# Moving squares, rows and factor sums from VectorE to GpSimd around the context part of a two-layer diffusion backbone

## What is computed

```
for layer in range(2):
    last = layer == 1
    sh1, sc1, g1, sh2, sc2, g2       = split(silu(c)     @ mod_w[layer] + mod_b[layer], 6)
    csh1, csc1, cg1, csh2, csc2, cg2 = split(silu(c_ctx) @ mod_w[layer] + mod_b[layer], 6)
    m_lat, m_ctx = mixer(...)                       # pooling + attention, then @ w_out
    h = h + g1 * m_lat
    f_lat = rmsnorm(h, norm_ffn_g) * (1 + sc2) + sh2
    h = h + g2 * ((silu(f_lat @ wg) * (f_lat @ wu)) @ wd)
    if not last:
        hc = hc + cg1 * m_ctx                       # the same for the context tokens
        ...
return h
```

## Time and profile before

| | |
|---|---|
| median of 3 runs | 3269.88 us (3264.45 to 3271.78) |
| the profiled execution's own time | 3270.94 us |
| its span, first to last instruction | 3268.8 us |
| PE busy | 3063.0 us, 94% of the span |
| POOL / DVE / ACT busy | 2193.1 / 1963.0 / 1089.5 us |
| mean granted TensorE clock | 0.968 of full speed |

### The profile page before, as it was taken

One profiled execution on the slowest core, in us unless ns is written; L12 is line 12 of the kernel. 1 busy time (PEld: TensorE's weight loads), 2 busy tenths in 40 slices (PEclk: granted clock), 3 DMA queues, 4 the chain that ended last, 5 costly groups with the idle time before them and its releaser, 6 DMA issues. The chain is left out here.

```text
span 3268.8 us, 44070 instructions
## 1 busy us (share of the span) xinstructions
PE 3063.0 (94%) x14302; PEld 2506.9 (77%) x14302; DVE 1963.0 (60%) x2625; ACT 1089.5 (33%) x1865; POOL 2193.1 (67%) x2250
## 2 busy tenths in 40 slices
PE   7998998989899999999798979999998999999999
PEld 6777876869777888888686757777776778888887
DVE  5585665787664454454435557777766765445454
ACT  4323675124530010110333446676772321010110
POOL 3584774520168888888633258888887688888884
PEclk9999998989899999999898979999998999999999
DMA  6367223458431111111212441111114211111112
GB/s 234 113 200 206 66 57 120 168 171 301 152 97 58 45 51 59 53 45 61 92 34 97 140 142 40 47 40 40 47 29 138 61 54 57 46 51 58 49 48 84
DMA packets 135064, 298.24 MB, mean 91 GB/s; under 512 B 36464, under 2 KB 69488, under 8 KB 134832
## 3 DMA queue, kind: packets, MB, share of 16 engines
q1 hardware_dynamic: 121776, 253.42, 24.7%
q10 hardware_dynamic: 13184, 43.52, 4.4%
HBM read 252.20 MB, written 44.63 MB: 91 GB/s over the span
## 5 line engine op out<-in xcount | busy, mean ns | idle before, releaser
L1546 POOL TENSOR_TENSOR a_pl<-a_p,a_ph 128x512 fp32r<-128x512 f32 x320 | 451.0, 1429 | 103.1 <-ACT a_p L1491 98.2
L164 PE MATMUL ps<-a_q,a_k 97*128 97x512 f32 x960 | 273.4, 398 | 1.2 <-POOL a_q L1565 1.2
L1490 ACT ACTIVATE a_ph<-ps 128x512 fp32r<-128x512 f32 x320 | 192.2, 601 | 178.8 <-PE ps L164 178.0
L1392 DVE TENSOR_REDUCE a_top<-ps 128x1 f32<-128x512 f32 x256 | 172.3, 687 | 95.3 <-PE ps L1316 95.3
L164 PE MATMUL ps<-hidden,whi 128*128 128x512 f32 x704 | 219.3, 393 | 5.0 <-issue 2.9
L164 PE MATMUL ps<-mixed_hi,l_whi 128*128 128x512 f32 (+1 forms) x544 | 208.9, 384 | 6.9 <-issue 2.9
L164 PEld LDWEIGHTS ps<-a_q,a_k 97*128 97x128 f32 x960 | 179.7, 191 | 38.2 <-issue 1.4
L2985 POOL TENSOR_TENSOR l_wlo<-l_raw,l_whi 128x512 fp32r<-128x512 f32 x154 | 199.4, 1295 | 12.8
L164 PE MATMUL ps<-mixed_lo,l_whi 128*128 128x512 f32 (+1 forms) x544 | 207.9, 382 | 0.0
L164 PE MATMUL ps<-mixed_hi,l_wlo 128*128 128x512 f32 (+1 forms) x544 | 207.8, 382 | 0.0
L3794 DVE SCALAR_TENSOR_TENSOR residual<-ps,mod,residual 128x512 f32<-128x512 f32 x176 | 132.0, 750 | 124.9 <-PE ps L164 124.9
(11 more groups left out here) (415 smaller groups left out, 8819.7 us busy)
## 6 DMA issues: line engine op xcount, KB each, us to landing
l_raw<-in_w_ffn SPq DMA_DIRECT2D x132, 512.0 KB, 3.7
raw<-in_w_ffn SPq DMA_DIRECT2D x66, 512.0 KB, 3.6
l_row<-in_mod_t ACTq DMA_DIRECT2D x48, 512.0 KB, 5.0
f_vraw<-in_mod_t ACTq DMA_DIRECT2D x24, 512.0 KB, 4.1
a_k<-scratch_k SPq DMA_DIRECT2D x32, 320.0 KB, 6.7
f_raw<-in_w_in SPq DMA_DIRECT2D x16, 512.0 KB, 5.4
l_raw<-in_w_out SPq DMA_DIRECT2D x16, 512.0 KB, 4.8
raw<-in_w_out SPq DMA_DIRECT2D x16, 512.0 KB, 4.5
```

Source lines behind the costliest of these rows:

```text
L164: last = nc.tensor.matmul(out, a, b, start=at == 0, stop=at == n - 1)
L1392: nc.vector.tensor_reduce(top[:, q:q + 1, c], e.ps[:, bank:bank + BANK], AX.X, ALU.max).then_inc(s["auxr"], 1)
L1490: nc.scalar.activation(ph[:, kk % 2, c], b, ACT.Exp).then_inc(s["exp"], 1)
L1546: nc.gpsimd.tensor_tensor(pl[:, kk % 2, c], p[:, kk % 2, c], ph[:, kk % 2, c].bitcast(F32), ALU.subtract).then_inc(s["pl"], 1)
```

## The change

1. **Squares.** `add(J)` moves in layer 0 from DVE to POOL, between the weight splits: both adds of block b stand ahead of the split of block b + 3 in pass 0.
2. **Rows.** Row products in pass 1 fall from 6 rows to 2 (`IN_MIX` 22 to 18), and the last 8 rows (`SHARED` = 40 to 47) are shared by POOL and ACT: POOL multiplies row and condition elementwise into `sq`, ACT copies `sq` onto itself with a sum along the row (`row_sum(n)`), one in each of pairs 0 to 5 and two in pair 6. DVE has 28 products in the context part as before. The loads of those rows stand on ACT's queue.
3. **Order on ACT.** In the context part `latent_units` comes one step later against `ctx_high`.
4. **Factor sums** move from DVE to POOL, in one block ahead of the latent part's weights; `second_low` and `third_low` are set elsewhere in pair 10.
5. **Tail.** The split of `latp` block 0 moves from POOL to ACT (high part, after square 3) and DVE (low part, after use 5).
6. **Layer 1.** One condition is loaded and silu'd, and each of the 8 rows takes one instruction.

```diff
 # mixer_ffn: SP and ACT conditions, DVE row
-                    for c in range(2):
+                    for c in range(1):
...
-                    matvec(e, dve, e.mod[:, 16 + own + r, :], raw_row[r % ROWS], cond, junk, s["vdone"], 2 * r)
+                    dve.wait_ge(s["vdone"], r)
+                    nc.vector.scalar_tensor_tensor(junk, raw_row[r % ROWS], 1.0, cond[0], ALU.mult, ALU.mult,
+                                                   accum_out=e.mod[:, 16 + own + r, 0:1]).then_inc(s["vdone"], 1)
 # layer0_rest
-    IN_MIX = 22
+    IN_MIX, SHARED = 18, 40
 # POOL (add is the same text as DVE's was)
                 for N in range(split, 2 * KT):
+                    b = N - RING
+                    if 0 <= b < KT:
+                        add(2 * b)
+                        add(2 * b + 1)
                     split_block(e, pool, mixp, 0, N, 1024)
+                    if b >= KT:
+                        add(KT + b)
+                for J in range(NJ - RING, NJ):
+                    add(J)
+
+                pool.wait_ge(s["add"], added(NJ - 1))
+                pool.wait_ge(s["conds"], 2)
+                for n in range(ROWS - SHARED):
+                    pool.wait_ge(sfull[n % 2], 16 * (n // 2 + 1))
+                    pool.wait_ge(s["summed"], n)
+                    nc.gpsimd.tensor_tensor(sq[:, :], shared_row[n % 2][:, :], cond[0][:, :], ALU.mult).then_inc(s["shared"], 1)
...
+                pool.wait_ge(s["nwhole"], 2 * KT)
+                pool.wait_ge(s["lo1"], 12)
+                for k in range(4):
+                    factor_sums(k)
...
-                pool.wait_ge(s["product"], pairs * PRODUCTS)
-                split_block(e, pool, latp, 0, 0, 1024)
 # PE
+                pe.wait_ge(s["tmp"], KT)
                 norm_sums(s, 1, False)
 # ACT
+                def row_sum(n):
+
+                    act.wait_ge(s["shared"], n + 1)
+                    shared_load(n + 2)
+                    nc.scalar.activation(sq[:, :], sq[:, :], ACT.Copy, accum_out=e.mod[:, 16 + OWN + SHARED + n, 0:1]).then_inc(s["summed"], 1)
...
                     ctx_high(q)
+                    latent_units(p, -1)
                     ctx_silu(2 * p)
-                    latent_units(p, 0)
                     if p:
-                        row(22 + 4 * p)
-                        row(23 + 4 * p)
                         ctx_high(q + 1)
+                        latent_units(p, 0)
+                        ctx_high(q + 2)
                         latent_units(p, 1)
-                        ctx_high(q + 2)
-                        latent_units(p, 2)
...
                     ctx_high(q + 2)
                     ctx_silu(2 * p + 1)
+                    latent_units(p, 3)
...
+                    if p < 7:
+                        row_sum(p)
+                    if p == 6:
+                        row_sum(7)
+                    ctx_high(q + 3)
+                    ctx_hidden(2 * p + 1)
                     latent_units(p, 4)
...
                     tail_square(x)
+                    if x == 3:
+                        act.wait_ge(e.raw_full[0], latp.filled(0, 0))
+                        act.wait_ge(s["product"], pairs * PRODUCTS)
+                        nc.scalar.activation(e.whi[:, 0, :], e.raw[:, 0, :], ACT.Copy).then_inc(e.split_hi, 1)
 # DVE
-                    if J not in (0, NA):
-                        add(J - 1)
-                    if J in (NA - 1, NJ - 1):
-                        add(J)
...
-                        if m < 6:
+                        if m < 2:
                             row_product(16 + m, 0)
...
                         if n == 27:
-                            dve.wait_ge(s["vdone"], products_done(ROWS - 1))
+                            dve.wait_ge(s["vdone"], products_done(SHARED - 1))
+                            dve.wait_ge(s["summed"], ROWS - SHARED)
                             add_bias(48, 64, 2, 2)
...
                     latent_use(pairs, x, of)
+                    if x == 5:
+                        dve.wait_ge(e.split_hi, latp.number(0, 0) + 1)
+                        nc.vector.tensor_tensor(e.wlo[:, 0, :], e.raw[:, 0, :], e.whi[:, 0, :].bitcast(F32), ALU.subtract)\
+                          .then_inc(e.split_done, 1)
```

More of the change, by code:

```diff
@@ L2205, in conditions @@
                 def conditions(x, of):
-                    act.wait_ge(s["cond"], 32 * (x + 1))
-                    for c in range(2):
+                    act.wait_ge(s["cond"], 16 * (x + 1))
+                    for c in range(1):
                         nc.scalar.activation(of[c], of[c], ACT.Silu).then_inc(s["conds"], 1)
@@ L2724, in layer0_rest @@
         raw_row = [piece_at(f"row{x}", 2 * x, 2) for x in range(4)]
+        shared_row = [piece_at(f"shared_row{x}", z, 2) for x, z in enumerate((21, 10))]
         cond = [piece_at(f"cond{x}", 15 + 2 * x, 2) for x in range(2)]
@@ L2754, in layer0_rest @@
         vfull = [sem(f"{name}_vfull{y}") for y in range(4)]
+        sfull = [sem(f"{name}_sfull{y}") for y in range(2)]
         e.ahead = nc.alloc_sbuf_tensor_at("h1_qn", [128, 4, NQ1], F32, offset=e.ahead_at)
@@ L2943, in _, with add @@
             def _(pool):
+                def add(J):
+                    P, m, c = jobs[J]
+                    a, w = CHUNKS[c]
+                    if m == 0:
+                        return
+                    x = added(J) - 1
+                    pool.wait_ge(s["sq"], x + 1)
+                    if m > 1:
+                        pool.wait_ge(s["add"], x)
+                    nc.gpsimd.tensor_tensor(total[:, a:a + w], total[:, a:a + w], sq[:, x % 2 * BANK:x % 2 * BANK + w], ALU.add)\
+                      .then_inc(s["add"], 1)
                 for N in range(split, 2 * KT):
+                    b = N - RING
+                    if 0 <= b < KT:
+                        add(2 * b)
+                        add(2 * b + 1)
                     split_block(e, pool, mixp, 0, N, 1024)
+                    if b >= KT:
[8 more added lines that the diff above has]
+                    nc.gpsimd.tensor_tensor(sq[:, :], shared_row[n % 2][:, :], cond[0][:, :], ALU.mult).then_inc(s["shared"], 1)
                 for u in range(KT, UNITS):
@@ L3391, in _ @@
                 act.wait_ge(s["cond"], 32)
+                for n in range(2):
+                    shared_load(n)
                 for c in range(2):
@@ L3414, in latent_units @@
                 def latent_units(p, x):
+                    if x < 0:
+                        p, x = p - 1, 5
                     if p in (7, 8):
@@ L3428, in second_and_third, with later_rows @@
                     factor_high(factor_[k, 5][:, :], whole_[k, 4][:, :], "t3hi")
+                def row_sum(n):
+                    act.wait_ge(s["shared"], n + 1)
+                    shared_load(n + 2)
+                    nc.scalar.activation(sq[:, :], sq[:, :], ACT.Copy, accum_out=e.mod[:, 16 + OWN + SHARED + n, 0:1]).then_inc(s["summed"], 1)
+                def later_rows(p, x):
+                    upto = 4 * p + 2 * x
+                    for r in range(IN_MIX + 4, SHARED):
+                        freed = 2 * (r - 4 - IN_MIX) + 1 if r - 4 < BOTH else r - 4 - 2 * IN_MIX + BOTH
+                        if upto - 2 < freed <= upto:
+                            row(r)
                 for p in range(pairs):
@@ L3447, in _ @@
                     ctx_hidden(2 * p)
-                    if p:
-                        row(24 + 4 * p)
-                        row(25 + 4 * p)
-                    latent_units(p, 3)
+                    latent_units(p, 2)
+                    if p == pairs - 1:
+                        second_and_third(2)
                     ctx_high(q + 2)
                     ctx_silu(2 * p + 1)
+                    latent_units(p, 3)
+                    if p == pairs - 2:
+                        second_and_third(0)
+                    later_rows(p, 1)
+                    if p < 7:
[4 more added lines that the diff above has]
+                    ctx_hidden(2 * p + 1)
                     latent_units(p, 4)
                     if p == pairs - 1:
-                        second_and_third(2)
                         second_and_third(3)
-                    ctx_high(q + 3)
-                    ctx_hidden(2 * p + 1)
-                    latent_units(p, 5)
                 for c in range(2):
@@ L3722, in gap @@
                             scaled(n + 1)
-                    elif p == 9:
-                        factor_sum(2 * x)
-                        factor_sum(2 * x + 1)
-                    elif x == 0:
-                        for n in range(12, 16):
-                            factor_sum(n)
-                    elif x == 3:
-                        second_low(0)
-                        second_low(1)
-                    elif x == 4:
-                        third_low(0)
-                        third_low(1)
+                    elif p == 10 and x in (1, 2):
+                        second_low(x - 1)
```

(6 more changed lines are left out.)

61 lines of the change are left out of this document (23 added, 38 removed).

## The result

The changed kernel takes 3249.65 us (median of 6 runs, 3247.45 to 3255.77) against 3270.14 for the kernel before (6 runs, 3263.9 to 3271.92): a ratio of 0.9947, 95% interval 0.9937 to 0.9956. It is faster by 20.5 us, where 9.8 were forecast. The profiled span is 3246.9 us against 3268.8.

A forecast was written before the change was run, and what follows sets the result against it. PE is busy 94% of the span, so only its stops or low-clock time can be won. Terms -2.6 + 12 + 3 + 5.2 - 17 + 1.5 - 6 - 5.9 = -9.8 give 3260.1 us on the median's scale, range 3238 to 3273.

The forecast's parts named there:

- rival A: Context pairs: POOL's shared products stay hidden, hand-over and pair 6 costs shrink to about +4; 3243 us, chance 0.26.
- Output projection, -2.6: Layer 0's output projection: sums 2.5 us later, but the 4.39 us stop before the first context block goes; -2.6 us.
- Hand-overs, +12 and +3: Behind pairs 0 to 5: POOL's product delays DVE's low part, PE starts 2.0 us late six times; 3 for low clock.
- Pair 6, +5.2: End of pair 6: two row sums make PE's next down 4.4 us late instead of 0.87, with 1.7 for the clock.
- Pairs 7 to 10, -17: Late context pairs: ACT and DVE overlap in the new order, winning back most of 21.8 us excess; -17 us.
- Latent part, +1.5: Start of the latent part: factor sums on POOL end 3.5 us late, and PE already waits for POOL; +1.5 us.
- rival C: Start of latent part: POOL's factor sums take over 25 us and make PE wait 14; 3274 us, chance 0.12.
- Tail, -6: Tail: POOL's additions start at once, the seventh ending near 1601.8 against 1607.8; -6 us, bounds -3 and -8.
- Layer 1, -5.9: Layer 1's output projection: without second row products DVE keeps up, the 4.13 us stop and slow matmuls go; -5.9 us.
- rival B: Every PE stop brings the low clock and port conflicts cost their upper bound; 3271 us, no change, chance 0.14.
- part 1: The output projection term: squares moved to POOL and rows taken off DVE, estimated together as -2.6 us.
- part 4: The term for pairs 7 to 10: ACT's new order and the factor sums' hold-ups, estimated together as -17 us.

The follow-up runs named there:

- e_keep: The changed kernel with squares and shared rows both back on DVE, the rest as changed: 3235.51 us, ratio 0.9905 to the kernel before.
- e_actold: The changed kernel with ACT's old order in the pairs and DVE's factor splits where they were, sums still on POOL: 3267.67 us, one run.
- e_sums: The changed kernel with the sixteen factor sums back on DVE in pairs 9 and 10, ACT's new order kept: 3250.09 us, one run.
- e_tail: The changed kernel with the tail's first weight block split by POOL again, ahead of the squares: 3260.53 us, one run.
- e_move: The changed kernel with ACT's row sums behind the SiLU that opens a pair, the eighth in the middle of pair 6: 3245.11 us, ratio 0.9937.
- e_move2: As e_move, but no sum in pair 0, and the sixth and eighth in the middle of pairs 5 and 6: 3242.92 us, ratio 0.9923.
- e_squares: The changed kernel with the adds of the squares back on DVE, POOL's eight row products kept: 3250.94 us, one run.

## Why the prediction was right

The forecast was faster by 9.8 us in a range from 3238 to 3273; 3249.65 lies in it, 2 us below the forecast's own range and at the upper end of rival A's, whose mechanism it is not. The gain is twice the one forecast, and that the total still lies in the range is owed to a range 35 us wide. The signs of all seven parts came out (the latent part's +0.2 is within the scatter of this stretch, 657.3 to 659.1), and the mechanisms are in the main those described; in span the sum was 12.1 us off: 6.9 in the projection and pairs 1 to 6, 2.0 in the tail, 2.3 in layer 1, 1.3 in the latent part and 2.3 in stretches whose code is the same, less 2.8 in pairs 7 to 10.

1. *Output projection, -2.6: measured -3.1* at the third context block (138.34 us behind the first matmul, 141.43 before), and -2.2 up to the first down without the hand-over's stop (-0.63 less 1.54). The sums came 1.6 late (2.5 forecast) and the stop of 4.39 went. But this was two effects: rows off DVE bring 3.6 to 5.7, squares on POOL cost 2.4 to 4.5. The forecast of the sums' stop, 13 to 16 us, was wrong: it fell to 9.57, since two stops of 1.50 and 1.81 behind POOL's splits came ahead of it.
2. *Hand-overs, +12 and +3: measured +9.5* (five periods longer by 1.59, and one stop of 1.54). The mechanism is the one described, down to POOL starting when DVE's row product ends. The term was mis-sized twice: the stop was taken as 2.0 and is 1.6, and the clock, taken as 3 from one stop of 2.21 us, costs nothing: it stays at 1.00 behind each of the six. A row sum of ACT also follows silu at once (741.62), not behind two issues, but POOL waits for DVE's row product anyway.
3. *Pair 6, +5.2: measured +3.3, and 1.6 more in pair 7.* The pair's own period grew from 18.11 to 21.43, with a stop of 4.14 (4.4 forecast). The 1.7 for the clock came as well, but behind the first down of pair 7: the granted clock from 844 to 847 us was 0.65, then 0.78, and that period is 1.6 us longer than in e_keep.
4. *Pairs 7 to 10, -17: measured -14.2,* of which +1.6 is pair 6's clock. ACT's order, with the new places of the factor splits, is worth 17.8, as e_actold shows. The step that failed is the price of the sums: 2.6 behind pair 9 was nearly right (its period is 2.2 above 17.19), but behind pair 10 only 1.3 was left for all else, and its period is 3.0 above; there PE stops 5.28 where it stopped 3.15.
5. *Latent part, +1.5: measured +0.2.* PE does wait longer at one place (4.23 us) and less elsewhere. The sixteen sums took 30.3 us (886.13 to 916.4), over the 25 from which rival C was to decide, and end 35.5 us behind the first down of pair 9, not 33; but POOL turns to the weights before PE is through with pair 10 (920.48), and the stop of 14 us did not come. e_sums, without sums on POOL, has the same latent part, so the forecast 1.5 is nothing. The price shows on DVE instead, in its longer splits and the 5.28 us of point 4.
6. *Tail, -6: measured -8.0,* the lower bound. The sums over the partitions came 4.9 us earlier, not 6, and no stop is left ahead of them, where 2 to 3 us were expected. What the forecast left out is the clock: behind the stop of 8.55 it was 0.50, and without the stop it is 1.00, which fits the 2.2 us up to the second sums. e_tail gives back 6.5 of the 8.0.
7. *Layer 1, -5.9: measured -8.2,* outside the bounds of -4 and -7. Of the 8.2, 6.3 lie ahead of the second sums, where the forecast stop and its slow matmuls are, and where the profiles agree within 1.6 us. The other 1.9 lie behind, where the same code differs by 5.6 us: they are no measured gain.

Rival A (products hidden) is out by the hand-over rows, rival B's low clock behind every stop by the windows behind them, and rival C by the latent part: the sums took longer than its 25 us, but its cost did not come. The page of the Trainium skill that the prediction drew on ("SBUF — State Buffer", section "Who interferes with whom") has an exclusive lock between DVE and GpSimd for instructions of DVE with both inputs in SBUF; the rows agree: 3.21 us for a product that takes 2.40 alone, and 2.54 to 3.42 for a split that takes 1.23.

The prediction's parts were stretches, not edits: part 1 held squares and rows in one sum, part 4 the order and the factor sums. So a total in the range hid that three of six edits are losses: 2.4 to 5.6 us for the squares, 6 to 11 for the rows with the clock behind pair 6, 3.9 for the factor sums.

## What to carry to other kernels

Elementwise work moved from DVE to POOL hardly left DVE's time in this kernel, where both read two SBUF tensors: DVE's remaining operations waited for POOL's, which are longer. Eleven adds of 13.7 us left DVE, and its row products became 12.2 us longer. Before moving such work, look at the order in which two engines hand blocks to each other (pairs 7 to 10: 17.8 us for the same instructions in another order), and undo a mixed change part by part even where it is faster as a whole.

## What the runs showed of the hardware

- A POOL product of 128x1024 took 2.40 us alone and 3.20 or 3.21 when it came up behind a DVE operation; DVE's next split, 1.23 us alone, then took 2.54 to 3.42. The exclusion costs on both sides, and moving the product to another place of the pair (e_move, e_move2) did not remove it.
- Stops of PE of 1.5 us left the granted clock at 1.00 (2.4 GHz) behind six of six hand-overs; behind the stop of 4.14 us it was 0.65 for 3 us. The six kernels with that stop (4.14 or 4.15 us) have 0.50 to 0.65 there, the six changed kernels whose stop is 0.65 to 1.26 us have 1.00. The low clock made the next pair 1.6 us longer, 2.8 in e_squares.
- In e_move ACT waited 4.76 us for a weight block's DMA before 750.25, though the kernel before, with a period of 17.19 us, shows no stop of PE there. Why that block came late stays open.
